# Query/key square sums in two single passes with a residue from GpSimd, the final norm on GpSimd, value evictions on ScalarE, depthwise taps moved up, joined masks

## The reference

```python
x = rmsnorm(h, final_norm_g)                     # end of the first block
h = rms_norm(x, norm1_g)
q, k, v, glu_a, glu_b = split(h @ w_in)          # 3 x 512 and 2 x 512 columns
q, k = rms_norm per head of 64 columns           # 8 heads
attn = stick_breaking_attention(q, k, v)         # strictly causal, blocks of 128
#   z = q k / 8;  log-sigmoids of z and -z;  reversed running sums;  exp;  times v
c = glu_a * sigmoid(glu_b)
c = causal_depthwise_conv(c, 31 taps)            # 512 channels
c = silu(layer_norm(c))
x = x + concat([attn, c]) @ w_out
```

## Time and profile before

| | us |
|---|---|
| median of 3 runs | 1237.2 |
| lowest and highest | 1235.92, 1237.4 |
| the profiled execution's own time | 1236.73 |
| its span | 1235.0 |
| PE busy | 1223.8 |
| DVE, POOL, ACT busy | 601.2, 574.2, 505.1 |

### The profile page before, as it was taken

The page is one execution under the profiler, slowest core; times in us unless marked ns, Lnnn a source line. Parts: engine busy times, 40 slices in busy tenths (PEclk is TensorE's granted clock), DMA queues, the critical chain, the costliest instruction groups (busy, mean ns, idle before and its releaser), DMA issues.

```text
span 1235.0 us, 16489 instructions
## 1 busy us (share of the span) xinstructions
PE 1223.8 (99%) x5598; PEld 1004.6 (81%) x5598; DVE 601.2 (49%) x877; ACT 505.1 (41%) x674; POOL 574.2 (46%) x465
## 2 busy tenths in 40 slices
PE   9999999999999999999999999999999999999998
PEld 7888888888888888888888886768888888888887
DVE  6782435434653166414575879785334213321431
ACT  7532543343443144313473237666333223332331
POOL 5775553233445344453465441134454444444444
PEclk9999999999999999999999999999999999999999
DMA  8343332112333322232133321102232323223222
GB/s 298 124 145 126 118 103 69 51 69 68 102 102 104 102 85 93 94 119 84 64 124 104 101 86 51 35 18 85 71 104 98 117 88 102 86 85 120 81 76 81
DMA packets 34034, 118.41 MB, mean 96 GB/s; under 512 B 4032, under 2 KB 4160, under 8 KB 33856
## 3 DMA queue, kind: packets, MB, share of 16 engines
q1 hardware_dynamic: 33696, 117.49, 28.6%
q10 hardware_dynamic: 288, 0.24, 0.1%
HBM read 115.61 MB, written 2.10 MB: 95 GB/s over the span
## 4 chain that ended last, share of the span: by engine, by line
PE 95%; ACT 2%; DVE 1%; POOL 1%; issue 1%; DMA 0%; SPq 0%; POOLq 0%; ACTq 0%; DVEq 0%
PE ps L1240 29%; PE ps L1241 29%; PE ps L1242 29%; PE ps L1562 1%; PE ps L1407 1%; PE ps L1545 1%; PE ps L1298 1%; PE ps L1297 1%; PE ps L1296 1%; PE ps L1518 0%; PE ps L1306 0%; POOL w_lo L363 0%; PE ps L1603 0%; ACT slab L654 0%; POOL squares L431 0%
## 5 line engine op out<-in xcount | busy, mean ns | idle before, releaser
L363 POOL TENSOR_TENSOR w_lo<-w_raw,w_hi 128x512 fp32r<-128x512 f32 x430 | 555.3, 1315 | 621.8 <-ACT w_hi L464 355.7
L1240 PE MATMUL ps<-xg_hi,w_hi 128*128 128x512 f32 x960 | 375.7, 391 | 0.0
L1242 PE MATMUL ps<-xg_hi,w_lo 128*128 128x512 f32 x960 | 373.7, 389 | 0.0
L1241 PE MATMUL ps<-xg_lo,w_hi 128*128 128x512 f32 x960 | 373.6, 389 | 0.0
L1240 PE MATMUL ps<-y_hi,w_hi 128*128 128x512 f32 (+1 forms) x608 | 230.8, 380 | 0.0
L1241 PE MATMUL ps<-y_lo,w_hi 128*128 128x512 f32 (+1 forms) x608 | 229.8, 378 | 0.0
L1242 PE MATMUL ps<-y_hi,w_lo 128*128 128x512 f32 (+1 forms) x608 | 229.8, 378 | 0.0
L1240 PEld LDWEIGHTS ps<-xg_hi,w_hi 128*128 128x128 f32 x960 | 180.3, 188 | 37.8 <-issue 0.8
L1242 PEld LDWEIGHTS ps<-xg_hi,w_lo 128*128 128x128 f32 x960 | 180.2, 188 | 37.5
L1241 PEld LDWEIGHTS ps<-xg_lo,w_hi 128*128 128x128 f32 x960 | 180.3, 188 | 37.3 <-issue 0.5
L464 ACT ACTIVATE w_hi<-w_raw 128x1024 fp32r<-128x1024 f32 x124 | 130.5, 1053 | 126.0 <-PE ps L1242 126.0
(11 more groups left out here) (210 smaller groups left out, 1058.1 us busy)
## 6 DMA issues: line engine op xcount, KB each, us to landing
w_raw<-weights SPq DMA_DIRECT2D x199, 512.0 KB, 3.3
w_raw<-weights SPq DMA_DIRECT2D x16, 384.0 KB, 2.9
out_t<-h SPq DMA_DIRECT2D x8, 256.0 KB, 2.1
h<-x_t SPq DMA_DIRECT2D x3, 512.0 KB, 8.4
slab<-mem_t SPq DMA_DIRECT2D x2, 512.0 KB, 10.1
slab<-mats_in SPq DMA_DIRECT2D x1, 1024.0 KB, 7.3
w_raw<-weights SPq DMA_DIRECT2D x2, 256.0 KB, 3.9
h<-x_t SPq DMA_DIRECT2D x2, 256.0 KB, 4.4
```

The source lines that it names most:

```text
L363: nc.gpsimd.tensor_tensor(w_lo[:, s, half], w_raw[:, s, half], w_hi[:, s, half].bitcast(F32), ALU.subtract).then_inc(done, 1)
L1240: pe.matmul(out, w[0], x[0], start=first, stop=False)
L1241: pe.matmul(out, w[0], x[1], start=False, stop=False)
L1242: return pe.matmul(out, w[1], x[0], start=False, stop=last)
```

## The change

The square sum of a query/key tile: ACT squares the tile twice, once as before to `sq` in f32 and once to an fp32r tile (`qk_square_hi`). POOL subtracts the second from the first and gets the residue. PE multiplies `pair_ones_r` (fp32r) by both parts in two fp32r matmuls where there was one f32 matmul. The final norm goes from DVE to POOL, one tile behind each weight block from the fourth block of the gated unit on; its gain is applied by DVE in the residual. The values are evicted by ACT; DVE waits for it and gives the bank semaphores by four small memsets. Eight taps move in front of the query/key stage. The masks of a head are three matmuls instead of four. `pair_ones` shares memory with `later_sums`, and `squares` with a new fp32r view of it.

```diff
@@ POOL
-            weights_lo_for(GLU, WOUT2 - GLU)
+            for b in range(GLU, V2 + 4):
+                weights_lo_next(b)
+                m = b - GLU - 3
+                if m == 0:
+                    pool.wait_ge(spread_copied, NORM_FINAL + 1)
+                if 0 <= m < DT:
+                    nc.gpsimd.tensor_tensor(h[:, m, :], h[:, m, :], final_bc[:], ALU.mult).then_inc(final_done, 1)
+            for t in range(8):
+                pool.wait_ge(qk_square, t + 1)
+                pool.wait_ge(qk_square_r, t + 1)
+                nc.gpsimd.tensor_tensor(sq_lo[:, t % 2, :], sq[:, t % 2, :], qk_square_hi(t).bitcast(F32),
+                                        ALU.subtract).then_inc(qk_square_lo, 1)
+                weights_lo_next(QK + t)
@@ ACT
             for b in range(V2, QK):
                 weights_hi_for(b)
+            act.wait_ge(rcol_ready, NORM_ONE + 1)
+            act.wait_ge(blocks_done, V2 + 4)
+            for t in range(ST):
+                nc.scalar.activation(v2[:, t, :], ps[:, t, :], ACT.Copy, scale=rcol[:, NORM_ONE, t:t + 1]).then_inc(v2_ready, 1)
@@ ACT, qk_squares_of
-                nc.scalar.activation(sq[:, t % 2, :], (q2, k2)[t % 2][:, t // 2, :], ACT.Square).then_inc(qk_square, 1)
+                values = (q2, k2)[t % 2][:, t // 2, :]
+                nc.scalar.activation(sq[:, t % 2, :], values, ACT.Square).then_inc(qk_square, 1)
+                nc.scalar.activation(qk_square_hi(t), values, ACT.Square).then_inc(qk_square_r, 1)
                 weights_hi_for(QK + t)
@@ DVE, residual
+                    if norm == NORM_TWO:
+                        nc.vector.scalar_tensor_tensor(out=new, in0=h[:, m, :], scalar=col("final_norm_g", m), in1=new,
+                                                       op0=ALU.mult, op1=ALU.add).then_inc(summed, 1)
@@ DVE
+            nc.vector.tensor_copy(pair_ones_r[:], pair_ones[:]).then_inc(rounded, 1)
-                conv_taps((3, 5, 5, 33)[i])
-            dve.wait_ge(blocks_done, V2 + 4)
-            for t in range(ST):
-                nc.vector.tensor_scalar(v2[:, t, :], ps[:, t, :], rcol[:, NORM_ONE, t:t + 1], None, ALU.mult).then_inc(banks_freed, 1)
+                conv_taps((3, 5, 5, 41)[i])
+            dve.wait_ge(v2_ready, ST)
+            for t in range(ST):
+                nc.vector.memset(tiny[:, 3, t:t + 1], 0.0).then_inc(banks_freed, 1)
             qk_apply(2)
-            conv_taps(8)
+            conv_taps(6)
             qk_apply(3)
-            conv_taps(5)
+            conv_taps(4)
             qk_apply(4)
-            conv_taps(6)
+            conv_taps(5)
             qk_apply(6)
-            conv_taps(5)
+            conv_taps(4)
             qk_apply(7)
-            conv_taps(12)
+            conv_taps(9)
             ln_centre()
-            final_norm(range(DT))
@@ PE
-                pe.wait_ge(qk_square, t + 1)
-                pe.matmul(ps[:, QK_BANK[t], :], pair_ones[:], sq[:, t % 2, :], start=True, stop=True).then_inc(qk_sums, 1)
+                pe.wait_ge(qk_square_r, t + 1)
+                pe.matmul(ps[:, QK_BANK[t], :], pair_ones_r[:], qk_square_hi(t), start=True, stop=False)
+                pe.wait_ge(qk_square_lo, t + 1)
+                pe.matmul(ps[:, QK_BANK[t], :], pair_ones_r[:], sq_lo[:, t % 2, :], start=False, stop=True).then_inc(qk_sums, 1)
@@ PE, pair_scores
-                    for tile in (0, 1, 3, 2):
-                        bank, at, n = TILES[tile]
-                        mm = pe.matmul(ps[:, 3 * (hd % 2) + bank, at:at + P], ident_r[:], far_below_r[:], start=False, stop=False,
-                                       skip_group_check=True)
-                    mm.then_inc(s_z, 1)
+                    bank = 3 * (hd % 2)
+                    pe.matmul(ps[:, bank, 0:P], ident_r[:], far_below_r[:], start=False, stop=False, skip_group_check=True)
+                    pe.matmul(ps[:, bank + 1, :].rearrange("p (a t) -> p a t", t=P)[:, 0:4:3, :], ident_r[:],
+                              far_below_r[:].rearrange("p (a t) -> p a t", a=1).broadcast_to([P, 2, P]), start=False, stop=False,
+                              skip_group_check=True)
+                    pe.matmul(ps[:, bank + 2, 0:P], ident_r[:], far_below_r[:], start=False, stop=False,
+                              skip_group_check=True).then_inc(s_z, 1)
```

More of the change, by code:

```diff
@@ L213, in build @@
         ones = sb("ones", [P, 1])
-        pair_ones = sb("pair_ones", [P, P])
         eps_q = sb("eps_q", [P, 1])
@@ L224, in build @@
         neg_ones = sb("neg_ones", [P, P])
-        squares = sb("squares", [P, 5 * SEQ])
+        with nc.sbuf_tensor("squares", [P, 5 * SEQ], F32) as squares:
+            pass
+        squares_r = sb("squares_r", [P, 5 * SEQ], F32R)
         stick_last = squares[:, 2 * SEQ:2 * SEQ + STICK]
-        sq = squares[:, 0:2 * SEQ].rearrange("p (a t) -> p a t", t=SEQ)
+        sq, sq_lo = (t[:, 0:2 * SEQ].rearrange("p (a t) -> p a t", t=SEQ) for t in (squares, squares_r))
         ssq = squares[:, 2 * SEQ:4 * SEQ].rearrange("p (a t) -> p a t", t=SEQ)
         later_sums = sb("later_sums", [P, 2, 3 * P])
+        pair_ones = later_sums[:, 0, 0:P]
+        pair_ones_r = sb("pair_ones_r", [P, P], F32R)
         rstd_bc = sb("rstd_bc", [P, SEQ])
@@ L277, in build @@
             sem(n) for n in ("ln_sum", "ln_sums", "ln_xc", "ln_log", "ln_rstd", "ln_norm", "ln_silu"))
-        qk_square, ln_square, ln_added, ln_total_ready = (sem(n) for n in ("qk_square", "ln_square", "ln_added", "ln_total_ready"))
+        v2_ready = sem("v2_ready")
+        qk_square, qk_square_r, qk_square_lo = (sem(n) for n in ("qk_square", "qk_square_r", "qk_square_lo"))
+        ln_square, ln_added, ln_total_ready = (sem(n) for n in ("ln_square", "ln_added", "ln_total_ready"))
         final_done = sem("final_done")
@@ L288, in stick_of, with qk_square_hi @@
             return stick_slab[:, hd % 4, :] if hd % 4 < 3 else stick_last
+        def qk_square_hi(t):
+            return (y_hi, y_lo)[t % 2][:, 7, :]
         FIRST, REST = slice(0, SEQ), slice(SEQ, STICK)
@@ L820, in residual @@
                     dve.wait_ge(blocks_done, first + m + 1)
-                    nc.vector.tensor_tensor(new, new, h[:, m, :], ALU.add).then_inc(summed, 1)
+                    if norm == NORM_TWO:
+                        nc.vector.scalar_tensor_tensor(out=new, in0=h[:, m, :], scalar=col("final_norm_g", m), in1=new,
+                                                       op0=ALU.mult, op1=ALU.add).then_inc(summed, 1)
+                    else:
+                        nc.vector.tensor_tensor(new, new, h[:, m, :], ALU.add).then_inc(summed, 1)
                     if m > 0:
@@ L1087, in final_rstd @@
                 copy_spread(final_bc[:], NORM_FINAL)
[L1089 to L1093, removed]
             tap_order = ([(0, j) for j in range(1, 4)] + [(0, 4), (0, 5), (0, 6), (0, 7)]
@@ L1192, in _ @@
             qk_apply(3)
+            conv_taps(4)
+            qk_apply(4)
             conv_taps(5)
-            qk_apply(4)
-            conv_taps(6)
             s_softplus(2)
@@ L1537, in pair_scores @@
                     pe.wait_ge(banks_freed, QK - USE_LAG)
-                    pe.wait_ge(rounded, 2)
                 for tile in (0, 1, 3, 2):
@@ L1621, in _ @@
             qk_block(1)
+            pe.wait_ge(rounded, 3)
             qk_sum(0)
```

## The result

The changed kernel takes 1239.56 us (median of 18, 1238.54 to 1240.63); the kernel before, timed beside it, 1236.8 (median of 18, 1235.92 to 1237.51). The ratio is 1.0022, interval 1.0016 to 1.0028: 2.8 us slower. The profiled execution of the changed kernel took 1238.54 us (span 1236.7), the fastest of its runs; that of before 1236.73. In 11 of the 18 runs the mean granted clock was 1.000, and their median is 1238.9; in the other 7 it was 0.998 or 0.999, with a median of 1239.97.

A forecast was written before the change was run, and what follows sets the result against it. PE bounds the kernel, busy 1223.8 of 1235.0 us. Terms +4.4 - 2.2 + 1.4 - 0.7 = +2.9 gave 1239.6 on the profiled execution, 1240.1 on the median; forecast 1239.9, range 1233.3 to 1242.4.

The forecast's parts named there:

- Part 1: PE work that goes: square sums 3.2 us, masks 0.8; together 4.0 us off PE, between 3.2 and 4.1.
- Part 2: Edits before 719 us: final norm on POOL in the gated unit and evictions on ACT cost 0; norm's bounds 0 to 10.
- (a): Attention stage's start: first input at 726.5, 3.3 us late; square sum 0 through at 730.5 instead of 729.33, +1.2.
- (b): Inputs 0 to 2: input 2 at 739.7 (old 736.03); first scores at 744.4 behind apply 1, +2.4 us.
- (c): Block 4 waits for apply 2 and starts at 749.3 instead of 745.36, +3.9 us.
- (d): Head 1's later_sums, held up by three POOL instructions, ready at 763.5 instead of 759.10, +4.4 us; PE's wait 2.5.
- (e): From there on: PE gets back 2.2 us, head 5's later_sums cost 1.4, last POOL wait of 0.7 goes; sum +2.9.
- Rival A: Residues hide, PE keeps its 4.0 us: 1233.2 us, chance 0.17; decides at (a), needing input 0 by about 724.
- the lock: SBUF-reading POOL and two-SBUF-input DVE instructions wait for each other: about 1.0 us on DVE per POOL instruction, POOL 0.25 to 0.4.
- the late start: DVE's first input of the attention stage at 726.5 instead of 723.22, 3.3 us late, behind eight more taps.

The follow-up runs named there:

- e9: e6 with the causal masks in four instructions as before the change; 1232.29 us, 0.74 over e6.
- e1: Changed kernel with square sums as before: one f32 matmul, no second square, no residue; 1235.48 us, ratio to before 0.9989.
- e2: Kernel before with only the two-pass square sums added (two squares, residue on POOL, two fp32r matmuls); 1239.48 us, ratio to before 1.0023.
- e3: Changed kernel without POOL's subtraction, PE multiplying the hi part twice, so sums are not the reference's; 1233.52 us, ratio to before 0.9975.
- e5: Changed kernel with POOL's residue replaced by two memsets that read no SBUF, sums not the reference's; 1233.92 us, ratio to before 0.9980.
- e4: Changed kernel with the eight moved taps back in their places of before; 1238.51 us, ratio to before 1.0015.
- e8: Changed kernel with the residue made by DVE, the order of taps kept as in the changed kernel; 1241.66 us, ratio to before 1.0038.
- e7: Changed kernel with the residue left on POOL and DVE's taps laid out anew; 1237.29 us, ratio to before 1.0004.
- e6: Changed kernel with the residue made by DVE and DVE's order laid out anew; 1231.55 us, ratio to before 0.9959.
- e10: e6 with the final norm back on DVE; 1232.14 us, ratio to before 0.9962.

## Why the prediction was right

The forecast was 1239.9, the time 1239.56; on the profiled executions +2.9 was said and 1238.54 - 1236.73 = +1.8 came, on the medians +2.8. The profiled execution of after was 0.6 us ahead before the stage began (w_hi of the last value block at 717.21, before at 717.78), and is the fastest of its runs. In the profiles of the twelve kernels this instruction starts between 717.21 and 718.52, and the two compared differ in PE's waits of the first 60 us (3.2 against 4.0 in all), so I take the 0.6 as chance; what follows corrects for it.

- **Part 1.** Sums: 0.23 + 0.23 us each in the chain of waits (764.96 and 765.20, scores at 765.43), as said. Masks 0.21 a pair, said 0.2; e9 has 0.74 in all.
- **Part 2.** The norm in the gated unit took 1.29 beside a pair of 2.55 and made no wait: 0, as said. Evictions on ACT took 2.40 for four; input 0 didn't wait for them.
- **(a)** Input 0 at 725.87, corrected 3.2 late, said 3.3. Eight taps took 7.21 us, said 5.3 + 1.9 = 7.2. The second matmul of sum 0 waited 1.34 and ended at 729.93, corrected +1.2, said +1.2.
- **(b)** Input 2 at 738.78: +3.3 corrected, said +3.7. Scores at 743.59 behind apply 1: +2.1, said +2.4 (744.4 - 742.06 is 2.3). Apply 1 was released by ACT's Exp, as said.
- **(c)** Block 4 at 748.33 behind apply 2: +3.5, said +3.9.
- **(d)** later_sums of head 1 ready at 762.24: +3.7, said +4.4; PE waited 2.15 for them, said 2.5. All three short instructions were held up there, 2.59 for two and 1.24 for the third, in DVE's timeline after:

```profile
758.38 2.59 DVE L1172 TENSOR_TENSOR later_sums<-slab 128x128 f32<-128x128 f32 x2
761.01 1.24 DVE L1175 TENSOR_TENSOR later_sums<-slab,later_sums 128x128 f32<-128x128 f32 x1
```

- **(e)** Head 5's later_sums, said ready at 807.7, were ready at 807.14, corrected 807.7 (2.61 and 1.24 for the three). PE waited 1.06 for them, which made it 1.2 later, said 1.4. The last wait for POOL fell from 0.7 to 0.2, and the last channel sum came at 830.52 instead of 828.77: +2.3 corrected, said +2.9.

(a) came within 0.1 us; from (b) on each step is 0.3 to 0.7 too long. Of the sum's terms, the +4.4 of (d) was 0.7 too large, the rest within 0.2: PE got back 2.2 as said. One wait isn't in the prediction, head 7's softplus, 1.5 instead of 0.6. It cost nothing net: PE came to it 0.8 earlier, as it no longer had the small idle times just before it, and went on as late as it had been (2.2 against before, uncorrected).

The mechanism is shown, but part of the closeness on the medians is luck. The prediction has no term for the clock. In the changed kernel's runs at a granted clock of 1.000 the median is 1238.9, 2.1 over the 1236.8 of before, as the corrected trace has it (+2.3). The 7 runs at a lower clock bring the median to +2.8, about as much as the sum was too long.

e1 and e2 show that the two passes alone carry the loss; e3 and e5, that it is the reading POOL instruction; e4, that the taps moved up are 1 us of it. Rival A didn't decide at (a) as was written. In e2 and e4 input 0 starts by 724 (723.96 and 723.71) and sum 0 doesn't wait, and still they lose 2.6 and 1.6 us, by the waits for the applies and later_sums. An input in time was needed for A and not enough. With the residue gone (e3) the kernel is 3.4 us faster than before, most of A's 4.0.

What the prediction had too simple: it spoke of the lock and of the late start as separate costs of the residue. e8 shows a third that it didn't name, the place in an engine's order: with the residue off POOL and nothing else laid out anew, nothing was won. e7 and e8 show a fourth, the clock that falls behind a long wait of PE.

## What to carry to other kernels

An engine that is busy for half the time isn't free: before giving it a short step of a chain, look at what it and its neighbour hold up with each other, in the rows where both already run, and at everything queued behind the step. When the bound engine loses work, its neighbours' deadlines move up by as much; the gain comes only with their order laid out for the new deadlines (e6 against e8: the same instructions, 10.1 us apart, some 3.4 of it by the clock that fell behind e8's waits). So when a kernel with a new wait is slower than its waits add up to, look at the granted clock behind them.

## What the runs showed of the hardware that was not expected

A POOL memset of 128x512 took 0.53 us, in the midst of DVE instructions with two SBUF inputs; a POOL subtraction of the same tile took 1.28 alone and up to 1.76 beside them.

With POOL busy without a pause, a row of DVE taps and POOL's subtractions go one in turn: the four taps from 733.10 took 5.76 us, 1.44 each, where three that POOL didn't hold up took 2.04, 0.68 each; POOL's pair took 3.42 to 3.44 instead of 2.54. Both engines lose, DVE about 0.8 a tap and POOL 0.45 an instruction.

The granted TensorE clock fell from 1.00 to 0.50 in four short stretches of three profiled executions, each during or soon after a wait of PE: of 3.02 us in e7, 2.29 and 2.09 in e8, 2.14 in e4. A stretch cost 1.7 to 2.7 us. The same wait isn't always followed by it: the profiled executions of the changed kernel (2.15) and of e2 (2.14) kept 1.00. The kernels that wait most are the ones whose runs show a mean clock of 0.997 to 0.999: 7 of 18 of the changed kernel, 3 of 8 of e2, 7 of 11 of e4, 10 of 11 of e7, 5 of 5 of e8, none of e1, e5, e6, e9 and e10. (One run of e3 showed 0.949 and took 1235.24, the longest of its 11.) This also widens their spread, 2.1 us for the changed kernel (18 runs) against 1.0 for e6 (5 runs). No run held the waits and changed the clock alone, so what makes it fall is not shown.
